# Stick-breaking attention inside a hybrid decoder layer: meta value product over 128 rows, logits pieces of two query tiles together

## The reference, cut to what matters

```
z       = (q @ k.T) / sqrt(64)            per head, all keys up to the query's block end
keep    = sigmoid(-z) where key < query, else 1
weight  = (1 - keep[t,s]) * product of keep[t,j] over s < j < t
out     = weight @ v
y       = out * gate
```

## Time and profile before

| what | value |
|---|---|
| median of three runs | 4387.74 us (4385.82 to 4387.82) |
| the profiled execution's own time | 4386.44 us |
| its span | 4384.7 us |
| busy: TensorE matmul / weight load | 4210.2 us (96%) / 3343.6 us (76%) |
| busy: VectorE / ScalarE / GpSimd | 2384.2 / 1663.3 / 801.4 us |
| mean granted TensorE clock | 0.984 of full speed |

### The profile page before, as it was taken

The page is one execution under the profiler, slowest core; times in us unless marked ns, Lnnn a source line. Parts: engine busy times, 40 slices in busy tenths (PEclk is TensorE's granted clock), DMA queues, the critical chain, the costliest instruction groups (busy, mean ns, idle before and its releaser), DMA issues. The chain is left out here.

```text
span 4384.7 us, 90811 instructions
## 1 busy us (share of the span) xinstructions
PE 4210.2 (96%) x35784; PEld 3343.6 (76%) x35784; DVE 2384.2 (54%) x3103; ACT 1663.3 (38%) x3296; POOL 801.4 (18%) x627
## 2 busy tenths in 40 slices
PE   7999999997999999997999999999899999999999
PEld 7888888885888888885555555555688888878887
DVE  6444444443444444443777777777466667743222
ACT  4222222223222222222666666666444444421111
POOL 2110111112111111110000000000256666610222
PEclk9999999998999999998999999999999999999999
DMA  2334333333333333334443343442233333355553
GB/s 93 109 117 120 120 108 114 99 115 108 118 111 115 112 107 111 114 106 105 84 94 76 74 94 63 85 93 62 74 114 99 99 99 99 97 182 177 188 188 129
DMA packets 486971, 479.74 MB, mean 109 GB/s; under 512 B 260610, under 2 KB 370818, under 8 KB 480914
## 3 DMA queue, kind: packets, MB, share of 16 engines
q1 hardware_dynamic: 475154, 450.33, 37.1%
q10 hardware_dynamic: 11520, 25.17, 1.6%
HBM read 305.45 MB, written 169.93 MB: 108 GB/s over the span
## 5 line engine op out<-in xcount | busy, mean ns | idle before, releaser
L1208 DVE TENSOR_TENSOR_SCAN kept<-keep,kept 128x512 f32<-128x512 f32 (+1 forms) x448 | 436.7, 975 | 73.6 <-ACT keep L1172 35.1
L1172 ACT ACTIVATE keep<-z 128x512 f32<-128x512 f32 (+3 forms) x704 | 343.8, 506 | 314.8 <-PE z L1104 282.4
L1626 POOL TENSOR_TENSOR off<-NT,tri 128x512 f32<-128x512 f32 x165 | 206.2, 1276 | 1242.2 <-ACT NT L1530 1242.2
L1114 PE MATMUL turned<-t_identity,kept 128*128 128x128 f32 (+1 forms) x2432 | 379.6, 278 | 26.0 <-DVE kept L1208 25.5
L1180 ACT COPY w<-turned 128x512 f32<-128x512 f32 (+4 forms) x704 | 362.6, 528 | 91.9 <-PE turned L1114 90.0
L1114 PEld LDWEIGHTS turned<-t_identity,kept 128*128 128x128 f32 (+1 forms) x2432 | 279.0, 136 | 139.8 <-ACT w L1180 52.1
L1205 DVE TENSOR_TENSOR_SCAN kept<-keep,hidden 128x512 f32<-128x512 f32 (+3 forms) x256 | 285.5, 1119 | 169.6 <-ACT keep L1172 167.6
L1142 PE MATMUL acc<-w,dv 128*64 128x512 f32 (+4 forms) x1280 | 377.5, 554 | 0.0
L1103 PE MATMUL z<-k_high,q_parts 128*128 128x512 f32 (+3 forms) x704 | 302.6, 431 | 30.7 <-DMA k_low<-scr_k_lo 26.4
L1103 PEld LDWEIGHTS z<-k_high,q_parts 128*128 128x128 f32 x704 | 135.2, 192 | 180.4 <-ACT keep L1172 88.3
L1104 PE MATMUL z<-k_low,q_parts 128*128 128x512 f32 (+3 forms) x704 | 252.4, 363 | 0.0
(11 more groups left out here) (552 smaller groups left out, 10742.4 us busy)
## 6 DMA issues: line engine op xcount, KB each, us to landing
w_raw0A<-in_w_main SPq DMA_DIRECT2D x42, 512.0 KB, 3.9
w_raw0B<-in_w_main SPq DMA_DIRECT2D x42, 512.0 KB, 3.9
w_raw1A<-in_w_main SPq DMA_DIRECT2D x41, 512.0 KB, 4.0
w_raw1B<-in_w_main SPq DMA_DIRECT2D x41, 512.0 KB, 3.8
KB<-scr_kb SPq DMA_DIRECT2D x33, 512.0 KB, 5.3
AR<-scr_ar SPq DMA_DIRECT2D x33, 512.0 KB, 5.3
y_raw<-scr_y SPq DMA_DIRECT2D x64, 256.0 KB, 4.9
merge<-scr_merge SPq DMA_DIRECT2D x64, 256.0 KB, 5.9
```

Of the source, the lines that this page charges most:

```text
L1114: mm = pe.transpose(turned[num % TB][0:size, P * r:P * r + P], kept[kept_in(g)][:, src:src + size], t["identity"][:, :])
L1172: act.activation(keep[num % KB][:, 0:size], z[num % ZB][:, 0:size], ACT.Sigmoid, scale=-DH ** -0.5).then_inc(keep_done, 1)
L1208: dve.tensor_tensor_scan(dst, data, data, kept[kept_in(g)][:, end:end + 1], ALU.mult, ALU.bypass).then_inc(scanned, 1)
L1626: pool.tensor_tensor(out, a, b, op).then_inc(s[name], 1)
```

## The change

Four things are changed, all of them in the attention stage.

- The meta value product uses 128 rows of the array. For this the dv rows 16 to 127 of the meta slot and all eight w tiles are set to zero once, by GpSimd, at the stage's start. SyncE waits for the two dv slots ahead of the first dv load, and ScalarE for all ten tiles ahead of its first copy.
- Logits pieces of query tiles qt and qt+1 are made together, as one entry of the list: first the two products with k_high over 128 rows into the two z banks, then the two with k_low over 64 rows each, the one in partitions 0 to 63 and the other in 64 to 127. The latter takes the queries' high part from a new tile q_again (64 partitions by 512 queries, one load for each group, two buffers). The product of the low query part with k_low is left out. Both z banks have to be empty before a pair starts. Where the second tile has a piece more than the first, it stands alone. That makes 320 pairs and 64 single pieces of 16 keys in place of 704 pieces.
- VectorE writes the sum of the halves directly into the y tile; the wait for the old store of y moves ahead of the sum. A scan waits for the earlier scan of its own query tile.
- The load of q_again is a new issue in SyncE's queue: for groups 0 and 1 ahead of head 0's load, for group 2 behind the first gates, and for group g+3 at the head of round g, behind a wait for the last logits of group g+1, and ahead of that round's wait for y.

The core of the diff:

```diff
-        for qt in range(GROUP * rank(g), GROUP * (rank(g) + 1)):
-            for k0, size in pieces_of(qt):
-                rows.append(("logits", g, qt, k0, size, nl))
-                nl += 1
+        for qt in range(GROUP * rank(g), GROUP * (rank(g) + 1), 2):
+            mine, next_tile = pieces_of(qt), pieces_of(qt + 1)
+            for i in range(len(next_tile)):
+                pieces = [(x, *some[i]) for x, some in ((qt, mine), (qt + 1, next_tile)) if i < len(some)]
+                rows.append(("logits", g, [(*piece, nl + j) for j, piece in enumerate(pieces)]))
+                nl += len(pieces)
...
                 if first == 0:
+                    sp.wait_ge(cleared, 2)
                     sp.dma_start(dv[u][0:META, 0, :], scratch["dv"][PAD:CHUNK, rows]).then_inc(v_sem, 16)
...
+            def load_again(g):
+                row, at = DH * head_of(g), 512 * rank(g)
+                sp.dma_start(q_again[g % 2][DH:P, :].bitcast(F32), scratch["q_hi"][row:row + DH, at:at + 512]).then_inc(again_in[g % 2], 16)
...
             sp.dma_start(hidden[:, :], io["hidden"]).then_inc(const_in, 16)
+            load_again(0)
+            load_again(1)
             for p, (first, last) in enumerate(FIRST_PARTS):
                 load(0, first, last, qk_first[p], v_first[p])
             load_gate(0)
             load_gate(1)
+            sp.wait_ge(logits_done, last_logits[0] + 1)
+            load_again(2)
             for g in range(GROUPS_ALL):
+                if g + 3 < GROUPS_ALL:
+                    sp.wait_ge(logits_done, last_logits[g + 1] + 1)
+                    load_again(g + 3)
                 sp.wait_ge(y_done, g + 1)
                 store_y(g)
...
-            def logits(g, qt, k0, size, num):
+            def logits(g, pieces):
                 u = head_of(g) % 2
-                if k0 + size == keys_of(qt) and qt % GROUP == 0:
+                if any(k0 + size == keys_of(qt) and qt % GROUP == 0 for qt, k0, size, _ in pieces):
                     queries_and_keys(g)
-                reach(pe, keep_done, num - ZB + 1)
-                out = z[num % ZB][:, 0:size]
-                queries = q_parts[u][:, P * qt:P * qt + P]
-                pe.matmul(out, queries, k_high[u][:, k0:k0 + size], start=True, stop=False)
-                pe.matmul(out, queries, k_low[u][:, k0:k0 + size], start=False, stop=True).then_inc(logits_done, 1)
+                    pe.wait_ge(again_in[g % 2], 16 * (g // 2) + 16)
+                reach(pe, keep_done, pieces[-1][3] - ZB + 1)
+                for qt, k0, size, num in pieces:
+                    pe.matmul(z[num % ZB][:, 0:size], q_parts[u][:, P * qt:P * qt + P], k_high[u][:, k0:k0 + size],
+                              start=True, stop=False)
+                for x, (qt, k0, size, num) in enumerate(pieces):
+                    part = slice(0, DH) if x == 0 else slice(DH, P)
+                    at = P * (qt % GROUP)
+                    queries = q_parts[u][part, P * qt:P * qt + P] if x == 0 else q_again[g % 2][part, at:at + P]
+                    pe.matmul(z[num % ZB][:, 0:size], queries, k_low[u][part, k0:k0 + size], start=False, stop=True).then_inc(logits_done, 1)
...
                 if c1 < 512:
-                    yield out[:, c1:512], dv[u][0:size, kt + 1, :], part[0:size, c1:512], kt <= 0, last and not own, not own
+                    yield out[:, c1:512], dv[u][:, kt + 1, :], part[:, c1:512], kt <= 0, last and not own, not own
...
                     act.wait_ge(turn_done, num + 1)
+                    if num == 0:
+                        act.wait_ge(cleared, 2 + WB)
...
-                    if not first:
-                        dve.wait_ge(scanned, num)
+                if not first:
+                    dve.wait_ge(scanned, scan_earlier[num] + 1)
...
-                    reach(dve, y_done, g)
-                    dve.tensor_tensor(total[:, :], acc[g % 2][0:DH, :], low_half[:, :], ALU.add).then_inc(total_done, 1)
+                    reach(dve, y_sent[g % 2], 16 * (g // 2))
+                    dve.tensor_tensor(y[g % 2][:, :], acc[g % 2][0:DH, :], low_half[:, :], ALU.add).then_inc(total_done, 1)
                     dve.wait_ge(total_done, g + 1)
                     dve.wait_ge(gate_in[g % 2], 16 * (g // 2 + 1))
-                    reach(dve, y_sent[g % 2], 16 * (g // 2))
-                    dve.tensor_tensor(y[g % 2][:, :], total[:, :], gate[g % 2][:, :], ALU.mult).then_inc(y_done, 1)
+                    dve.tensor_tensor(y[g % 2][:, :], y[g % 2][:, :], gate[g % 2][:, :], ALU.mult).then_inc(y_done, 1)
+
+        @block.gpsimd
+        def _(pool):
+            for tile in dv:
+                pool.memset(tile[:, 0, :], 0.0).then_inc(cleared, 1)
+            for tile in w:
+                pool.memset(tile[:, :], 0.0).then_inc(cleared, 1)
```

More of the change, by code:

```diff
@@ L961, in attention_phase @@
     FIRST_PARTS = [(0, GROUP), (GROUP, 2 * GROUP), (2 * GROUP, QT)]
-    last_logits = {e[1]: e[5] for e in order if e[0] == "logits"}
+    last_logits = {e[1]: e[2][-1][3] for e in order if e[0] == "logits"}
     last_values = {e[1]: e[3] for e in order if e[0] == "values"}
@@ L977, in attention_phase @@
         low_half = sb("low_half", [DH, 512])
-        total = sb("total", [DH, 512])
+        q_again = [sb(f"q_again{b}", [P, 512], F32R) for b in range(2)]
         gate = [sb(f"gate{b}", [DH, 512]) for b in range(2)]
@@ L984, in attention_phase @@
         acc = [ps(f"acc{b}", [P, 512]) for b in range(2)]
-        const_in = sem("a_const_in")
+        const_in, cleared = sem("a_const_in"), sem("a_cleared")
         qk_first, v_first = [[sem(f"a_{x}_first{b}") for b in range(len(FIRST_PARTS))] for x in ("qk", "v")]
@@ L991, in attention_phase @@
         half_done, total_done, y_done = sem("a_half"), sem("a_total"), sem("a_y")
+        again_in = [sem(f"a_again_in{b}") for b in range(2)]
         gate_in = [sem(f"a_gate_in{b}") for b in range(2)]
@@ L1017, in place @@
             return sum(keys_of(x) for x in range(GROUP * rank(g), qt))
+        scan_earlier, latest = {}, {}
+        for e in order:
+            if e[0] == "logits":
+                for qt, _, _, num in e[2]:
+                    scan_earlier[num] = latest.get((e[1], qt))
+                    latest[e[1], qt] = num
         def key_tile(kt):
@@ L1119, in products @@
                 u, half = head_of(g) % 2, DH * ((kt + 1) % 2)
-                _, size = key_tile(kt)
                 own = kt - GROUP * rank(g) >= 0
@@ L1168, in _ @@
                 if e[0] == "logits":
[L1169 to L1173, removed]
+                    for qt, k0, size, num in e[2]:
+                        act.wait_ge(logits_done, num + 1)
+                        reach(act, scanned, num - KB + 1)
+                        act.activation(keep[num % KB][:, 0:size], z[num % ZB][:, 0:size], ACT.Sigmoid,
+                                       scale=-DH ** -0.5).then_inc(keep_done, 1)
                 elif e[0] == "values":
@@ L1188, in _, with scan @@
         def _(dve):
+            def scan(g, qt, k0, size, num):
+                at = place(g, qt)
+                end = at + k0 + size
+                first = k0 + size == keys_of(qt)
+                dve.wait_ge(keep_done, num + 1)
+                if first and qt % GROUP == 0 and kept_earlier(g) is not None:
+                    dve.wait_ge(turn_done, last_values[kept_earlier(g)] + 1)
+                if not first:
+                    dve.wait_ge(scanned, scan_earlier[num] + 1)
+                data = keep[num % KB][:, 0:size][:, ::-1]
+                dst = kept[kept_in(g)][:, end - size:end][:, ::-1]
+                if first:
+                    dve.tensor_tensor_scan(dst, data, hidden[:, 512 - size:][:, ::-1], 1.0,
+                                           ALU.mult, ALU.max).then_inc(scanned, 1)
+                else:
+                    dve.tensor_tensor_scan(dst, data, data, kept[kept_in(g)][:, end:end + 1],
+                                           ALU.mult, ALU.bypass).then_inc(scanned, 1)
             dve.wait_ge(const_in, 16)
@@ L1191, in _ @@
                 if e[0] == "logits":
[L1192 to L1199, removed]
-                    if not first:
-                        dve.wait_ge(scanned, num)
[L1202 to L1209, removed]
+                    for piece in e[2]:
+                        scan(e[1], *piece)
                 elif e[0] == "sum":
```

## The result

The changed kernel takes 4855.15 us (median of four runs), the kernel before 4386.78: a ratio of 1.1064 [1.1051, 1.1077], or 468 us more. 4820 was forecast, with a range of 4690 to 4880. Direction and mechanism hold; the forecast is 35 us short. (The spans of the two profiled executions differ by 471 us.)

The account below looks back on a forecast made before the run. TensorE, busy 196 of 200 us, was taken to fill the attention stage. To the profiled 4386.4 us came +419 for stalls behind head loads in SyncE's queue and +18 for the rest: 4823, stated as 4820, range 4690 to 4880.

Parts of the forecast that it names:

- item 6: SyncE's queue: query-row load stuck behind head loads, TensorE waits 30.0 and 23.7 us per cycle; +419 us in all.
- item 7: Rest of the chain between stalls: meta -32, pairs +38, VectorE's gate wait -25, low clock +37; sum +18 us.
- Item 1: Meta value product over 128 rows: pair costs 1.0 instead of 2.0 us, -64 us where TensorE sets the time.
- Item 2: Low-key logits products in two row halves: a mode visit costs 0.42, saves 0.22 us; sum +67 us.
- item 4: VectorE sums straight into the y tile, its wait for the old store moving ahead of one add: 0.
- Item 5: Scans of the two tiles alternate, so a scan's wait on its forerunner goes; VectorE not the limit: 0.
- Items 3 to 5: GpSimd's zeroing of ten tiles at stage start, VectorE's sum into y, and alternating scans: each taken as 0.
- A: Rival: query copy in time as the head load's hold is short, row visits free; 4250 us, faster; chance 0.07.
- B: Rival: query copy in time, row visits cost what the projection's rows say; 4389 us, no change; chance 0.04.
- C: Rival: more is late, copy for group 8j+2 too, and low clock lasts longer; 4881 us; chance 0.06.
- D: Rival: stalls as said, but row visits free and clock loss small; 4705 us; chance 0.07.

Follow-up runs that it names:

- Experiment 4: Kernel before plus the 64 small query-row loads in SyncE's queue and TensorE's wait for them, logits reading nothing of them: 4811.3 us, 1.0973.
- experiment 5: Changed kernel with the dv_diag load of 127 rows cut into 112 and 15 rows on the same queue: 4380.7 us, 0.9991.
- experiment 6: Kernel before with the dv_diag load cut into 112 and 15 rows, without the meta product change: 4343.2 us, 0.9911.
- cut, meta (7): Kernel before with the meta product over 128 rows and the dv_diag load cut into 112 and 15 rows: 4298.8 us, 0.9809.
- experiment 1: Changed kernel with the query copy loaded whole with each head instead of group by group: 4442.7 us, 1.0125.
- experiment 11: Changed kernel plus products that nothing reads where TensorE waits for the query copy, to keep the clock up: 4839.8 us, 1.1025.
- experiment 8: Changed kernel with the cut dv_diag load and each pair's low-key products over 128 rows, one after the other: 4323.5 us, 0.9867.

## Why the prediction was right, and what it had too small

**The stalls (item 6) held.** Medians over six cycles, from start and end times in the traces, in us:

| stretch | before | forecast | after | wait alone (4) | cut load (5) |
|---|---|---|---|---|---|
| output 8j to logits 8j+4 | 25.0 | 55.0 | 55.2 | 55.2 | 27.7 |
| logits 8j+4 to output 8j+3 | 33.0 | - | 37.6 | 34.6 | 34.4 |
| output 8j+3 to logits 8j+7 | 31.8 | 55.5 | 55.4 | 55.4 | 30.7 |
| logits 8j+7 to output 8j+8 | 41.5 | - | 42.2 | 40.7 | 39.8 |

The two stalls of a cycle are right to 0.2 us, since they are a sum of issues in one queue and a landing time. At the start the first logits of group 4 came at 2154.5 where 2149.0 was forecast. With all cycles and the start, the delay adds up to 426 us where 419 was forecast.

**The rest on the chain (item 7) was too small.** I counted +18. The two unstalled stretches grew by 46 us in all, and with the 426 that makes, to 1 us, the 471 between the two profiled executions. Their sums over the whole trace, in us, tell the four parts:

| stretches | before | cut (6) | cut, meta (7) | cut, changed (5) | changed |
|---|---|---|---|---|---|
| eight from logits 8j+4 to output 8j+3 | 264.4 | 264.5 | 264.4 | 275.6 | 300.1 |
| seven from logits 8j+7 to output 8j+8 | 291.1 | 269.3 | 249.2 | 278.4 | 301.0 |

From each column to the next: the late gate that goes is worth -22 us (-25 forecast), the meta product -20 (-32), pairing and row halves +40 (+38), and the restart at the low clock +47 (+37). So the mis-sized terms are the meta product, which saves nothing in the first kind of stretch, and the clock. I took half speed for 6 us from the earlier trace rows, but in the changed kernel it lasted 9 us on average, 130 us behind all 15 stalls. Experiment 4 has only 66 us of low clock there, and its two sums are 28 us above those of experiment 6. So of the 44 us from 4811 to 4855 some 20 are pairs and meta, and about as much is the clock. Why it stays low for longer in the changed kernel is open.

**Item 1**, the term that failed most on its own: 64 us "where TensorE sets the time" turned into 10 alone and 44 with the load mended. I knew from the earlier trace rows that a gate comes late, but priced it as time to be gained and didn't ask what it does to a saving ahead of it.

**Item 2** had the sign and nearly the size: +67 forecast, +82 measured between experiments 7 and 5 (a difference that also holds items 4 and 5). But its parts differ: the row halves cost 57 us (0.12, 0.16, 0.23 and 0.17 an entry where I took 0.13, 0.15, 0.25 and 0.25), and pairing 25, which I hadn't priced at all. The 0.10 us before a weight load in another row mode is there again: in the changed kernel the low products' weight load starts 0.32 us after the second high product, where 0.23 is the steady step. The rule of the Trainium skill (TensorEngine Tiling, Key Properties) that a change of mode drains the engine was the one that counted. The up to 2x of the same page (Theoretical Speedup) holds here for the streams alone.

**Items 3 to 5** at 0 hold as far as the traces go. The zeroing took 4.0 us and was done at 2031, and the first copy came at 2053. The moved wait of item 4 took the place of the wait for the gate, as experiment 1 shows. Item 5 shows nowhere.

**The rivals.** A and B are out, since the hold was 52 us. With the hold at 22 us (experiment 5) the time is 4381, where B said 4389, but that is luck: B added -64 and +67, and the runs show -40 for the mended load, -44 for meta and +82 for the pairs. C's late copy for group 8j+2 costs nothing (with the clock held, the stretch behind 8j+7's logits is 39.7 us in experiment 11 as in 5), and of its longer low clock a third came true. D's free row visits are refuted by experiment 8, which is 57 us faster without them.

## What to carry to other kernels

Before adding a load to a queue that works in order, read what the queue is doing at the moment when the load is due, and compare its hold with the distance from what lets the load go to what needs it; buffers don't help where the issue itself is late. A saving only counts behind the last event that comes at a fixed time, so find that event first: here one load mended brought 40 us by itself and turned another saving from 10 us into 44. Row halves of the array didn't pay for one pair of products between others in full rows: it saved one stream of 0.22 us and still lost 0.12 on balance. By these two numbers a visit costs 0.34 us, so as an estimate two such pairs in one visit would gain 0.1; no run has tried it. And when a wait is added, count the low clock behind its end too: here each stall cost another 3 us on average.

## What was not expected of the hardware

- A DMA of 127 rows of 16 pieces of 256 bytes leaves a tail of 30 us at 15 to 16 GB/s; cut into 112 and 15 or 64 and 63 rows it leaves none of that kind, and cut into 14 and 113 it leaves one of 30 us again. The hold shows on the issue after it, not on the slow load.
- TensorE's granted clock fell to 0.50 after idle times of 1.6 to 2.3 us in ten of 15 restarts of experiment 11, with products back to back ahead of them, and stayed at 1.00 in the other five, after 1.3 to 1.8 us. The length of the idle time alone doesn't part the two: it fell after 1.64 us and stayed after 1.79.
